# Norm chains ahead of weight splits, row blocks in halves and latent squares as steps of their own, in a two-block transformer kernel

## What is computed

```python
x = layer_norm(DN_ALPHA * x + f, ln3_g[l], ln3_b[l])          # end of the first block
u = rms_norm_2(h, norm_w[i])                                  # input norm of each layer of the second
proj = u @ in_w                                               # ssm: xs, bc, dt, z    mla: cq, mz
q = (rms_norm_2(c_q, q_norm_w) @ uq_w)                        # latents 0 to 2
kv = (rms_norm_2(c_kv, kv_norm_w) @ ukv_w)                    # latents 3 and 4
o = causal_block_attention(q_full, k_full, v, MLA_QK_DIM ** -0.5)
```

## Time and profile before

| | |
|---|---|
| runs of the kernel, us | 1790.49, 1795.08, 1796.35 (median 1795.08) |
| the profiled execution, us | 1792.13 |
| its span, first to last instruction, us | 1790.3 |
| PE busy, us | 1714.2 |
| VectorE, ScalarE, GpSimd busy, us | 866.8, 768.6, 745.4 |
| mean granted TensorE clock | 0.983 |

### The profile page before, as it was taken

The page is one execution under the profiler, slowest core; times in us unless marked ns, Lnnn a source line. Parts: engine busy times, 40 slices in busy tenths (PEclk is TensorE's granted clock), DMA queues, the critical chain, the costliest instruction groups (busy, mean ns, idle before and its releaser), DMA issues.

```text
span 1790.3 us, 23237 instructions
## 1 busy us (share of the span) xinstructions
PE 1714.2 (96%) x8928; PEld 1378.2 (77%) x8928; DVE 866.8 (48%) x1773; ACT 768.6 (43%) x1315; POOL 745.4 (42%) x1009
## 2 busy tenths in 40 slices
PE   8999799999999999998989999999999999999998
PEld 7876567877888888887766777777777777787876
DVE  6358973533632212225655653355554544535356
ACT  6545553532642323214444554254444553534443
POOL 5735222232365555552454555455441343323330
PEclk9999799999999999999988999999999999999999
DMA  8422001121222232321211222221221211212201
GB/s 301 179 92 74 21 1 47 54 68 68 71 95 95 94 105 85 116 83 48 94 48 48 71 71 71 75 84 53 72 73 61 72 49 55 79 61 84 83 1 48
DMA packets 25814, 136.50 MB, mean 76 GB/s; under 512 B 2623, under 2 KB 7999, under 8 KB 12008
## 3 DMA queue, kind: packets, MB, share of 16 engines
q1 hardware_dynamic: 25704, 135.02, 22.0%
HBM read 132.88 MB, written 2.12 MB: 75 GB/s over the span
## 4 chain that ended last, share of the span: by engine, by line
PE 80%; DVE 8%; ACT 7%; POOL 2%; issue 2%; DMA 1%; DVEq 0%; ACTq 0%; POOLq 0%; SPq 0%
PE ps L1377 77%; PE ps L1381 3%; ACT whi L1853 1%; POOL wlo L2763 1%; DMA raw<-wall 1%; ACT tmp L1853 1%; DVE mx L2278 1%; ACT L1853 1%; DVE XS L2275 1%; DVE tmp L2275 1%; ACT ESG L1853 1%; POOL ECG L2794 1%; DVE LG L2275 1%; PE ps L1385 0%; ACT ECG L1853 0%
## 5 line engine op out<-in xcount | busy, mean ns | idle before, releaser
L2763 POOL TENSOR_TENSOR wlo<-raw,whi 128x256 fp32r<-128x256 f32 (+1 forms) x924 | 670.3, 761 | 857.5 <-ACT whi L1853 857.5
L1377 PE MATMUL ps<-XH,whi 128*128 128x512 f32 (+1 forms) x1144 | 301.9, 384 | 9.7 <-ACT XH L1853 9.7
L1853 ACT ACTIVATE whi<-raw 128x2048 fp32r<-128x2048 f32 (+4 forms) x135 | 231.4, 1719 | 173.8 <-PE ps L1377 165.0
L1377 PE MATMUL ps<-XL,whi 128*128 128x512 f32 (+1 forms) x1144 | 281.5, 368 | 0.0
L1377 PE MATMUL ps<-XH,wlo 128*128 128x512 f32 (+1 forms) x1144 | 280.4, 367 | 0.0
L1377 PEld LDWEIGHTS ps<-XH,whi 128*128 128x128 f32 x1144 | 200.9, 191 | 55.3 <-issue 10.3
L1377 PEld LDWEIGHTS ps<-XL,whi 128*128 128x128 f32 x1144 | 203.5, 190 | 36.5
L1377 PEld LDWEIGHTS ps<-XH,wlo 128*128 128x128 f32 x1144 | 203.5, 190 | 35.8
L2367 DVE TENSOR_TENSOR R<-ps,R 128x512 f32<-128x512 f32 (+1 forms) x128 | 79.9, 624 | 257.8 <-PE ps L1377 256.9
L1377 PE MATMUL ps<-BH,whi 128*128 128x512 f32 (+1 forms) x480 | 131.5, 390 | 1.2 <-ACT BH L1853 1.2
L1377 PE MATMUL ps<-BL,whi 128*128 128x512 f32 (+1 forms) x480 | 125.1, 376 | 0.8 <-DVE BL L2690 0.8
(11 more groups left out here) (310 smaller groups left out, 2703.8 us busy)
## 6 DMA issues: line engine op xcount, KB each, us to landing
raw<-wall SPq DMA_DIRECT2D x107, 1024.0 KB, 4.7
raw<-wall SPq DMA_DIRECT2D x11, 512.0 KB, 3.4
raw<-wall SPq DMA_DIRECT2D x8, 576.0 KB, 3.6
raw<-wall SPq DMA_DIRECT2D x4, 768.0 KB, 4.1
BFL<-scr SPq DMA_DIRECT2D x2, 1024.0 KB, 6.9
outT<-R SPq DMA_DIRECT2D x16, 128.0 KB, 1.8
MEM<-memT SPq DMA_DIRECT2D x2, 512.0 KB, 5.0
XTA<-x SPq DMA_DIRECT2D x2, 512.0 KB, 9.5
```

Of the source, the lines that this page charges most:

```text
L1377: return nc.tensor.matmul(o_, l, r_, start=start, stop=stop, skip_group_check=True)
L1853: return nc.scalar.activation(o_, i_, func, bias=bias, scale=scale)
L2763: t = tt(wlo[u % NSPL][:, c], raw[u % NRAW][:, c], f32(whi[u % NSPL][:, c]), ALU.subtract)
```

## The change

- `half_in`: for each half of the tokens and each unit, part 0 of both tiles, then part 1 of both.
- `token_turn`, case "f": after "ap" of block 2 six steps of the inner norm are emitted instead of three (three of squares, the inverse root, and two of three tiles each), ahead of the product of block 3's second half and of both splits; the last norm step comes behind the first split and ahead of "st" of block 3 and the second split.
- the latents: the squares leave "lt" and become steps "lq". Those of latents 0 to 2 are emitted behind the last product of `half_in`, ahead of its last split; "lt" 0 follows after the first part of the third cq unit instead of the second, then "lq" 3 and 4; "lt" 3 follows after the first part of the first mz unit.
- `paced` takes a list of least counts; for p = 1 it is (1, 3, 4) instead of (0, 1, 2), so that after the second product of the pair three attention steps are out (logits 0, a pause, and turn 0 with logits 1) instead of two.

```diff
-                slots += [("open", ("ls", k), "tmp"), ("close", ("ls", k), [("p_lt", k - k0 + 1)])]
+                slots.append(("close", ("ls", k), [("p_lt", k - k0 + 1)]))
...
+            "lq": lambda k: ({"a_ls": 1}, [("open", ("ls", k), "tmp")]),
...
-                    for m in range(2):
-                        emit("pj", u, m, j, 0)
-                        yield
-                        emit("pj", u, m, j, 1)
-                        yield
+                    for part in range(2):
+                        for m in range(2):
+                            emit("pj", u, m, j, part)
+                            yield
...
                 go(out_)
                 emit("ap", e, 2)
-                go(inside[0], 3)
+                go(inside[0], 6)
                 go(out_)
+                run(inside[0])
                 emit("st", e, 3)
                 run(out_)
-                run(inside[0])
...
-        between(half_out("so", 1, 8, 2), [rms_norm("r1", j) for j in range(2)] + [1.6], half_in(("cq", "cq")))
+        def latents_in():
+            for i, _ in enumerate(half_in(("cq", "cq"))):
+                if i == 15:
+                    for k in range(3):
+                        emit("lq", k)
+                yield
+
+        between(half_out("so", 1, 8, 2), [rms_norm("r1", j) for j in range(2)] + [1.6], latents_in())
...
-        weave(project("cq", 2, 8), emits("lt", 0), 0.9)
+        weave(project("cq", 2, 8), chain(emits("lt", 0), emits("lq", 3), emits("lq", 4)), 1.0)
...
-        def paced(main, steps, side, n):
+        def paced(main, steps, side, n, early=(0, 1, 2)):
...
-                while done < max(n * (i + 1) // steps, min(i, 2)):
+                while done < max(n * (i + 1) // steps, early[min(i, 2)]):
...
-        weave(gate_in(0), emits("lt", 3), 0.9)
+        weave(gate_in(0), emits("lt", 3), 1.0)
...
-                paced(chain(*before_, pair_in(p)), 10 if p > 1 else 6, heads_of, 8)
+                paced(chain(*before_, pair_in(p)), 10 if p > 1 else 6, heads_of, 8, (0, 1, 2) if p > 1 else (1, 3, 4))
...
+            def lq(k):
+                buf = taken(e, "ls", k)
+                u = first["cq"] + k // 2
+                e.wait_ge(*on("a_qc", *last_part(u, k % 2, 1 if info[u][3] == "in" else None)))
+                act(buf[:, :], QC[:, k, :], ACT.Square).then_inc(S("a_ls"), 1)
+
             def lt(k0):
                 k1 = {0: 3, 3: 5}[k0]
-                for k in range(k0, k1):
-                    buf = taken(e, "ls", k)
-                    u = first["cq"] + k // 2
-                    e.wait_ge(*on("a_qc", *last_part(u, k % 2, 1 if info[u][3] == "in" else None)))
-                    act(buf[:, :], QC[:, k, :], ACT.Square).then_inc(S("a_ls"), 1)
```

More of the change, by code:

```diff
@@ L657, in latent @@
             for k in range(k0, k1):
-                slots += [("open", ("ls", k), "tmp"), ("close", ("ls", k), [("p_lt", k - k0 + 1)])]
+                slots.append(("close", ("ls", k), [("p_lt", k - k0 + 1)]))
             slots += [("open", ("lr", k0), "tmp"), ("close", ("lv", k0), [("a_lr", 1)]),
                       ("close", ("lr", k0), [("d_ln2", 0)])]
-            return {"a_ls": k1 - k0, "p_lt": k1 - k0, "a_lr": 2, "d_ln2": k1 - k0, "a_qh": k1 - k0, "d_ql": k1 - k0}, slots
+            return {"p_lt": k1 - k0, "a_lr": 2, "d_ln2": k1 - k0, "a_qh": k1 - k0, "d_ql": k1 - k0}, slots
         def mla_logits(p, n):
@@ L1779, in lt @@
                 for k in range(k0, k1):
-                    e.wait_ge(*on("a_ls", "lt", k0, i=k - k0 + 1))
+                    e.wait_ge(*on("a_ls", "lq", k))
                     mm(o_[:, :], on1[:, :], slot("ls", k)[:, :], k == k0, k == k1 - 1).then_inc(S("p_lt"), 1)
@@ L2261, in scalar_program @@
                       ex=ex, tu=tu, rc=rc, ss=ss, dq=dq, mv=mv, uv=uv, ce=ce, ct=ct, cv=cv, dc1=dc1, sx=sx,
-                      gate=gate, g0=g0, g2=g2, g3=g3, g4=g4, lt=lt, kn=kn, vv=vv, zs=zs, qk=qk, pt=pt, pv=pv))
+                      gate=gate, g0=g0, g2=g2, g3=g3, g4=g4, lq=lq, lt=lt, kn=kn, vv=vv, zs=zs, qk=qk, pt=pt, pv=pv))
         def vector_program(e):
```

## The result

The changed kernel takes 1782.95 us (median of 4 runs, 1779.89 to 1784.7), the kernel before, run beside it, 1794.96 (4 runs). The ratio is 0.9932, 95% interval 0.9914 to 0.995: faster by 0.5 to 0.9%. The forecast was 1786.5 us, inside 1780.5 to 1792.5. The two profiled executions are 1792.13 and 1784.70 us (spans 1790.3 and 1782.9): 7.4 us apart, against a sum of 8.6.

The account below looks back on a forecast made before the run. PE, busy 1714.2 of 1790.3 us, bounds the kernel, so only its idle or low-clock time can shrink. 4.1 + 1.5 + 2.6 + 2.0 - 1.6 = 8.6 us, against the median 1795.08, gives 1786.5 us, range 1780.5 to 1792.5.

Parts of the forecast that it names:

- The head of "f": First half of the norm in token turn "f": root and six tiles first, second transposes start 4.1 us earlier.
- (B): Rival: the head of "f" does not pay, leaving a gain of 4.5 us, 1790.6 us; chance 0.22.
- The second half: Second half of the norm in "f": front half of m1 goes first, so tile 7 arrives in time; gain 1.5 us.
- Row blocks elsewhere: Turns 1 and 2 and the norm near 1330 us: 0 us, with one 2.8 us wait at 1334 us.
- The latents: Latent norms: squares ahead of the split remove two waits of 1.30 us before the sums; gain 2.6 us.
- Attention: First attention steps: the 3.08 us wait for PMT becomes a 1.05 us wait at the turn; gain 2.0 us.
- The clock: Gaps in "f" (3.3 us) and at 1334 us (2.8 us): one of two drops the clock, costing 1.6 us.
- PE's busy time would fall: Sign, whole kernel: PE's busy time falls by the low clock that goes; no size given.
- (A): Rival: the sum of the terms holds, whole kernel at 1786.5 us; chance 0.50.
- (C): Rival: both gaps keep the high clock and a fall further on goes too, 1783.3 us; chance 0.14.
- (D): Rival: each wait returns under another name, whole kernel at 1795 us; chance 0.08.
- (E): Rival: slower, long low clock behind the two new gaps and one further on, 1798.1 us; chance 0.06.

Follow-up runs that it names:

- e1: Kernel before with only the norm order of turn "f" changed: inverse root and six normed tiles ahead of the splits; 1786.94 us, ratio 0.9953.
- e2: Kernel before with only the row blocks in halves; 1792.42 us, ratio 0.9979.
- e9: Changed kernel with row blocks only in a unit's second half, tiles as before in its first half; 1781.63 us, ratio 0.9934.
- e7: Changed kernel with 22 unread matmuls in the 2.93 us gap before the second transposes of "f"; 1783.48 us, ratio 0.994.
- e5: The kernel before, unchanged, timed and traced again; 1793.2 us, ratio 1.0002.
- e8: Changed kernel with three splits moved later, two in "f" and one at the first latent weights; 1781.08 us, ratio 0.9928.
- e4: Kernel before with only the pace of the first attention steps changed; 1791.33 us, ratio 0.9977.
- e10: e8 with 20 unread matmuls ahead of the second transposes of "f"; 1778.38 us, ratio 0.9914.
- e12: e10 with 23 and 11 more unread matmuls in the gaps of the decay sums behind "f"; 1776.6 us, ratio 0.9905.
- e11: Kernel before with 28 unread matmuls in its 3.63 us gap in "f"; 1795.31 us, ratio 1.0016.
- e6: The changed kernel, unchanged, timed and traced again; 1784.32 us, ratio 0.9953 to the kernel before.

## Why the prediction was right, and where it was not

**The head of "f", 4.1 us.** The mechanism and the size. From the first sum of squares to the second transposes it was 24.83 us and is 20.93: 3.90. The two rows don't begin alike, though: the one of before starts with the first of sixteen transposes, the one of after with the third. The third stood at 25.05 before, so like for like the gain is 4.12. The root came at 822.84, which less the 1.23 us of shift is 821.61 (821.6 said). The norm tiles came at 0.86 us, not at the copied 0.73, which the work behind covers. From Ln to the transposes it took 2.11 us (2.14 said). The gap is 2.93 us (3.3 said). e1 reaches its fourteen transposes 20.97 us behind the sum without the row blocks, so the 4.1 belong to the order of the norm, as the prediction had it. Rival (B), a head that doesn't pay, is out.

**The second half, 1.5 us.** 1.42 in the changed kernel, 1.43 in e2. No product of its back halves waits for XH.

**Row blocks elsewhere, 0.** Right at r1: one wait of 2.68 us (2.8 said) and no shift. In turns 1 and 2 the gap of 1.80 us stands unchanged before the second transposes. Wrong by omission in the first half of "f": the prediction counted the blocks there as part of the gain, and e9 shows that without them the stretch is 2.2 us shorter, by the place of the low clock.

**The latents, 2.6 us.** 3.04, in every kernel that has this part. The term was undersized: I took the idle time that the rows name, 1.30 twice, and each stop cost 1.5. Groups of four such products start 0.91 us apart though each takes 1.07, an overlap of 0.16 that a stop loses, and the sum behind the stop took 2.81 us instead of 2.74.

**Attention, 2.0 us.** 1.89. The wait that replaced the 3.08 was put at 1.05. PE was ready at 1401.95 (1407.45 less a shift of 5.50) and the second transpose of the turn began at 1403.01, 1.06 later; the first fell in between, so the idle time reads 0.20 and 0.36.

**The clock, 1.6 us.** This step failed in size, and in its reasoning on place. One fall of the two came, as forecast, behind the gap in "f". It cost 2.8 us from the third transpose to the root of the second half (9.46 us before, 12.24 now) and 2.7 by e7. I had taken the price from turn 2, where the low clock lasted 3.4 us; in "f" it lasted 6.8. And the sum left out that the kernel before had a fall in "f" too, mostly under waits. The claim that PE's busy time would fall was wrong for the same reason (1714.2 to 1717.2): the low clock did not go, it moved from under ScalarE's waits to PE's own work.

The low clock behind "f" shows that from the other side. The kernel before has two low stretches there, one on each side of its wait for ZS. The wait in the kernel before, and two windows of its repeat, e5, where the wait is 3.69:

```profile
956.59 0.66 PE L1381 MATMUL ps<-KT,XS 128*128 128x128 f32 x2 [3.67 <-ACT ZS L1853]
```

```profile
938.00:943.00 5.00, 3.59 (x5) 0.66 0.00 0
955.00:963.00 8.00, 6.01 (x17) 0.57 0.00 0
```

In e8 the wait is 0.42, and in the changed kernel, at 0.54 for the 15 us from 937, there is none, and no low clock behind it. Counted from the end of "f" and matched with the rows of the kernel before, the changed kernel is 1.1 us late at 941 and 5.5 late at 950: the slow stretch did cost PE 4.4 us. The wait that is gone gives 3.8 back, and the fall that used to follow it 2.8, so at 963 it is 1.2 us early. This is where the 0.91 us behind "f" come from, and the 3.7 us that the waits for ZS lost: from the place of the falls, not from a step of the change. The Trainium skill, TensorE: Matmul & The Clock Gate, section "HAM oscillation", counts the penalty as low-clock time times one half. By that, as an estimate, the 15 us at 0.54 cost about 7 and the two stretches of the kernel before about 5, so the changed kernel would lose 2 us on it there; it gained 2.3, and the wait of 3.67 makes up most of the difference. In "f", where no wait follows, the rule gives 3.4 for 8 us at 0.57 and e7 shows 2.7, which nearly agrees. So the rule prices PE's work, and a wait behind that work has to be taken off.

**Rivals.** (A), the sum, is what happened: 7.4 us in the profiled pair, 9.7 and 12.0 by two pairs of medians. The nearness of 8.6 to 7.4 is in part luck: the terms in their own places give 7.7, with the clock 1.2 dearer and the latents 0.4 better than forecast, and the other two stretches, +1.23 and -0.91, nearly cancel. (C) would fit the first median, 1783.3 against 1782.95, but its reason does not hold in either traced execution: the gap in "f" lost the clock. (A) plus the scatter of the runs would also give the first median, and four runs cannot say more. (D) is out: no wait came back under another name at its old length. (E) is out as a cost: the clock kept its level at r1, and the fall further on that did grow, from 937 on, stood ahead of the wait for ZS.

What stays open is why the same gap keeps the clock in one execution and loses it in the next, how the falls are shared among the runs of a median, and why the medians of e1 to e4 lie further below the kernel before than their traces show.

## What to carry to other kernels

When an engine's queue holds a long job ahead of a short one that the matmul engine waits for, put the short one first; the time came back here as 4.1, 3.0, 1.9 and, at r1, 1.8 us, and the traces show it even where medians can't. Price a gap by what runs behind it: work that follows without a wait pays for the low clock, waits hide it. Where gaps can't be closed, unread matmuls that fit them kept the clock there (e7, e10, e12), but filling one gap while others follow may only move the fall, as in the one trace of e11.

## What the hardware showed that I had not expected

- Gaps of equal length differ: 2.68 us kept the clock at r1 and 2.67 us lost it (e7); 3.08 us kept it in attention in the kernel before, and the same gap was followed by a low stretch in e1 and e2 (+1.5 us each).
- A low stretch outlasted its gap by far: the 14 us at 0.51 from 893 in the changed kernel hold gaps of 3.10 and 1.48 us, but PE was at work for 10.79 of them.
- The runs of one program on one chip spread over 10 us (0.6%), with a mean granted clock of 0.980 to 0.985. The spread differs from kernel to kernel (e6: 10.7 us in 9 runs, e10: 7.1 in 5, e12: 3.6 in 4, e9: 2.6 in 5), and these runs do not show that filled gaps make it smaller.
- The clock can stay low while PE is fully at work: in the kernel before it is at 0.50 from 900 to 907.9 us, and PE is busy for all 7.9 of them.
- Extra matmuls can make a kernel faster: e12 has 54 of them, some 7 us of PE's work, and the lowest median. Its interval is clear of the changed kernel's second timing and overlaps with those of e10 and e8; what the filler alone gives is seen in the traces, 1.6 us in e10's "f" and 2.2 behind e12's.
